# Two half-block products and their sums of the first two up blocks, computed beside the tail's last tiles

## What is computed

```
x = x + rms_norm(mix @ w_out)                       # tail, lane a
u = rms_norm(x)
x = x + rms_norm(cross_attn(u, mem_kv, w_mq, w_mo)) # tail, lanes b, c, d
u = rms_norm(x)                                     # tail, end of lane d: u_T
h = u @ ffn_w_up                                    # ffn: 2 x 2816 columns
c = conv_b + sum(hp[:, k:k + T] * conv_w[k])        # width 3
y = (silu(c[..., :2816]) * c[..., 2816:]) @ ffn_w_down
```

## Time and profile before

| | us |
|---|---|
| median of 3 runs | 3021.24 |
| lowest and highest | 3016.79, 3022.23 |
| the profiled execution, its own time | 3014.63 |
| its span (first to last instruction) | 3012.9 |
| tail stage in the trace | about 1865 to 2147.6 |
| ffn stage in the trace | 2147.6 to about 2717 |

### The profile page before, as it was taken

One profiled execution on the slowest core, in us unless ns is written; L12 is line 12 of the kernel. 1 busy time (PEld: TensorE's weight loads), 2 busy tenths in 40 slices (PEclk: granted clock), 3 DMA queues, 4 the chain that ended last, 5 costly groups with the idle time before them and its releaser, 6 DMA issues. The chain is left out here.

```text
span 3012.9 us, 42602 instructions
## 1 busy us (share of the span) xinstructions
PE 2831.8 (94%) x15048; PEld 1970.8 (65%) x15048; DVE 1307.9 (43%) x2969; ACT 639.2 (21%) x1540; POOL 486.3 (16%) x355
## 2 busy tenths in 40 slices
PE   8999999998989989899999799998699999999998
PEld 5777777765656656566666666555588888874443
DVE  4111123233542597265666344234466666662321
ACT  2111000001322244244444211244111111110010
POOL 1100100003320343100000100011233333320011
PEclk9999999998999999999999899899899999999999
DMA  7644364426983643521111554200234343404020
GB/s 197 138 83 92 90 181 122 133 86 181 261 254 94 176 155 104 183 86 41 46 35 51 179 191 144 83 35 29 80 100 145 109 142 108 146 20 169 2 84 28
DMA packets 343542, 345.04 MB, mean 115 GB/s; under 512 B 61001, under 2 KB 310025, under 8 KB 341982
## 3 DMA queue, kind: packets, MB, share of 16 engines
q1 hardware_dynamic: 298706, 259.32, 29.7%
q10 hardware_dynamic: 44662, 83.46, 8.3%
HBM read 289.37 MB, written 110.01 MB: 133 GB/s over the span
## 5 line engine op out<-in xcount | busy, mean ns | idle before, releaser
L294 PE MATMUL d_ps<-d_w,mixer_u_T 128*128 128x288 f32 (+2 forms) x2048 | 581.4, 431 | 17.7 <-PEq L145 10.3
L294 PEld LDWEIGHTS d_ps<-d_w,mixer_u_T 128*128 128x128 f32 x2048 | 381.6, 193 | 159.0 <-issue 39.2
L298 PE MATMUL d_ps<-mixer_u_T,d_w 128*128 128x352 f32 x1152 | 398.6, 481 | 20.7 <-DVE d_ob L318 11.3
L298 PEld LDWEIGHTS d_ps<-mixer_u_T,d_w 128*128 128x128 f32 x1152 | 208.0, 195 | 127.1 <-issue 39.5
L3376 PE MATMUL ffn_ps<-up_u_T,up_up_w 128*128 128x264 f32 x704 | 163.2, 391 | 2.3 <-DVEq L3509 2.3
L3376 PE MATMUL ffn_ps<-up_u_T,ffn_S 128*128 128x264 f32 x704 | 163.8, 386 | 0.0
L3376 PE MATMUL ffn_ps<-ffn_T,up_up_w 128*128 128x264 f32 x704 | 163.8, 386 | 0.0
L318 DVE COPY d_ob<-d_ps 128x288 f32<-128x288 f32 (+3 forms) x144 | 66.3, 462 | 218.4 <-PE d_ps L294 164.8
L3376 PEld LDWEIGHTS ffn_ps<-up_u_T,up_up_w 128*128 128x128 f32 x704 | 135.7, 193 | 26.4 <-DVEq L3509 2.7
L3070 PE MATMUL down_Y<-down_w,feed_g_T 128*128 128x512 f32 x352 | 151.9, 593 | 0.0
L3376 PEld LDWEIGHTS ffn_ps<-ffn_T,up_up_w 128*128 128x128 f32 x704 | 133.8, 190 | 22.9
(11 more groups left out here) (519 smaller groups left out, 3863.3 us busy)
## 6 DMA issues: line engine op xcount, KB each, us to landing
out_dil_sample<-cache_dil_w ACTq DMA_DIRECT2D x10, 3264.0 KB
up_up_w<-ffn_w_up SPq DMA_DIRECT2D x44, 512.0 KB, 5.2
cmp_rows<-cache_nsa_kv SPq DMA_DIRECT2D x128, 128.0 KB
graw<-d_ob SPq DMA_DIRECT2D x72, 176.0 KB
mix_gate<-graw SPq DMA_DIRECT2D x24, 528.0 KB, 6.0
dils_qb<-proj SPq DMA_DIRECT2D x24, 512.0 KB, 7.4
d_w<-w_in SPq DMA_DIRECT2D x24, 512.0 KB, 6.2
ssd_x<-proj SPq DMA_DIRECT2D x29, 384.0 KB, 4.4
```

The costliest lines, as they stand in the source:

```text
L294: mm = pe.matmul(bank(u)[0:rows, 0:cols], self.u_T[:, k, r0:r0 + rows], self.view(i)[:, k, :], start=(k == 0), stop=(k == DK - 1))
L298: mm = pe.matmul(bank(u)[:, 0:cols], self.view(i)[:, k, x, :], self.u_T[:, k, c * third:(c + 1) * third], start=(k == 0), stop=(k == DK - 1))
```

## The change

In the tail stage, lanes of one step (PE and ACT) are added that make, for blocks 0 and 1 (m = 0, 1), the product P1 (j = 0) of both x into ps_a, copy it to SBUF, then accumulate P2 on top of it (j = 1) and copy the sum P1 + P2. A DVE lane of one step makes two token combinations (T0 and T1 for x = 0), and a POOL lane of four steps makes the four weight combinations of block 0. The results lie in rows of g_T that lane a has finished with. In the ffn stage blocks 0 and 1 skip P1 and P2; block 0 takes its S and the x = 0 input of P6 from the tail's results; the sums C11 become copies; POOL's S of block 0 is gone there, and `clear` stands behind the memsets; the T operations take x = 1 first; the loops of PE, ACT and DVE begin one turn later, with the first turn written out; ACT issues the first turn's two cache transfers ahead of the sigmoid.

```diff
--- before.py
+++ after.py
@@ -3356,11 +3356,13 @@
                                 P5=(lambda slot: A(slot, 1, 0), lambda x: t_of(0, x)), P3=(lambda slot: S[:, 2], lambda x: B(1, 1, x)),
                                 P4=(lambda slot: A(slot, 1, 1), lambda x: t_of(2, x)))
                 weights_made = dict(P6=3, P3=4)
-                inputs_made = dict(P6=(2, 4), P7=(5, 6), P4=(7, 8))
-
-                def block_products(it, slot):
+                inputs_made = dict(P6=(4, 4), P7=(5, 6), P4=(7, 8))
+
+                def block_products(it, slot, begun=False):
                     pe.wait_ge(w_in[slot], it * 32 + 32)
                     for i, (p, x) in enumerate(ORDER):
+                        if begun and p in ("P1", "P2"):
+                            continue
                         q, y = ORDER[(i + RING) % NP]
                         if q == "P1":
                             pe.wait_ge(held, n_of(it, slot, 2, 1 + y))
@@ -3369,16 +3371,26 @@
                             pe.wait_ge(summed, added(it, slot, name) - (NA if i < RING else 0))
                         if p in weights_made:
                             pe.wait_ge(S_made, n_of(it, slot, 4, weights_made[p]))
-                        if p in inputs_made:
+                        lhs, rhs = operands[p]
+                        weights, tokens = lhs(slot), rhs(x)
+                        if begun and slot == 0 and p in ("P6", "P7", "P3"):
+                            weights = begun_weights(g_T)[:, ("P6", "P7", "P3").index(p)]
+                        if begun and slot == 0 and p == "P6":
+                            if x == 0:
+                                tokens = begun_tokens(g_T, 1)
+                            else:
+                                pe.wait_ge(T_made, 2)
+                        elif p in inputs_made:
                             pe.wait_ge(T_made, inputs_made[p][x])
-                        lhs, rhs = operands[p]
                         for k in range(KH):
-                            mm = pe.matmul(bank(p, x)[:, 0:quarter], lhs(slot)[:, k, :], rhs(x)[:, k, :],
+                            mm = pe.matmul(bank(p, x)[:, 0:quarter], weights[:, k, :], tokens[:, k, :],
                                            start=(k == 0), stop=(k == KH - 1))
-                        mm.then_inc(product, 1)
-
-                pe.sem_inc(product, NP)
-                with pe.Fori(0, NB // 2) as it:
+                        mm.then_inc(product, 5 if begun and slot == 0 and (p, x) == ORDER[-1] else 1)
+
+                pe.sem_inc(product, NP + 4)
+                for slot in range(2):
+                    block_products(0, slot, True)
+                with pe.Fori(1, NB // 2) as it:
                     stand(pe, aside)
                     for slot in range(2):
                         block_products(it, slot)
@@ -3405,10 +3417,15 @@
                     for out, cs in parts_of(it * 2 + slot, 0):
                         act.activation(out, cs, ACT.Sigmoid).then_inc(gated, 1)
 
+                act.sem_inc(held, 4)
                 for out, src, n in windows:
                     act.dma_start(out[:, n * TURNS:, :], src[:, n * TURNS:, :]).then_inc(moved, 16)
-                hold(0, 0)
-                with act.Fori(0, TURNS) as it:
+                for out, src, n in windows:
+                    act.dma_start(out[:, 0:n, :], src[:, 0:n, :]).then_inc(moved, 16)
+                gate(0, 0)
+                hold(1, 0)
+                gate(0, 1)
+                with act.Fori(1, TURNS) as it:
                     for out, src, n in windows:
                         act.dma_start(out[:, bass.ds(it * n, n), :], src[:, bass.ds(it * n, n), :]).then_inc(moved, 16)
                     hold(it, 1)
@@ -3435,8 +3452,17 @@
                 def made(it, slot, p, x):
                     dve.wait_ge(product, n_of(it, slot, NP, after(p, x)))
 
-                def first_sums(it, slot):
+                def first_sums(it, slot, begun=False):
                     dve.wait_ge(packed, n_of(it, slot, 2, 2))
+                    if begun:
+                        held_P1, corner = (a.rearrange("p (x c) -> p x c", x=2) for a in begun_sums(g_T, slot))
+                        for x in range(2):
+                            at = pad + quarter * x
+                            dve.tensor_copy(h[:, slot, 0, at:at + quarter], corner[:, x, :]).then_inc(summed, 1)
+                        for x in range(2):
+                            made(it, slot, "P6", x)
+                            add(kept[:, 1, x, :], held_P1[:, x, :], bank("P6", x)[:, 0:quarter])
+                        return
                     for x in range(2):
                         dve.wait_ge(held, n_of(it, slot, 2, 1 + x))
                         made(it, slot, "P2", x)
@@ -3496,9 +3522,9 @@
                         dve.wait_ge(gated, n_of(it, slot, 2, 1 + i))
                         dve.tensor_tensor(out, out, cs, ALU.mult).then_inc(silu, 1)
 
-                def both(now_at, before):
+                def both(now_at, before, begun=False):
                     convolve(*before, 0)
-                    first_sums(*now_at)
+                    first_sums(*now_at, begun)
                     convolve(*before, 1)
                     gate(*before)
                     second_sums(*now_at)
@@ -3507,9 +3533,9 @@
                 dve.sem_inc(st_copied, 1)
                 dve.sem_inc(convolved, 12)
                 dve.sem_inc(summed, NA)
-                for x in range(2):
+                for i, x in enumerate((1, 0)):
                     dve.tensor_tensor(t_of(0, x), B(0, 1, x), B(0, 0, x), ALU.subtract).then_inc(T_made, 1)
-                    dve.wait_ge(T_made, 2 * x + 1)
+                    dve.wait_ge(T_made, 2 * i + 1)
                     dve.tensor_tensor(t_of(1, x), B(1, 1, x), t_of(0, x), ALU.subtract).then_inc(T_made, 1)
                 for x in range(2):
                     dve.tensor_tensor(B(0, 1, x), B(1, 1, x), B(0, 1, x), ALU.subtract).then_inc(T_made, 1)
@@ -3517,10 +3543,12 @@
                 for x in range(2):
                     dve.tensor_tensor(t_of(2, x), B(1, 0, x), t_of(1, x), ALU.subtract).then_inc(T_made, 1)
                 dve.wait_ge(ready, 2)
-                first_sums(0, 0)
+                first_sums(0, 0, True)
                 second_sums(0, 0)
                 states(0, 0)
-                with dve.Fori(0, NB // 2 - 1) as it:
+                both((0, 1), (0, 0), True)
+                both((1, 0), (0, 1))
+                with dve.Fori(1, NB // 2 - 1) as it:
                     both((it, 1), (it, 0))
                     both((it + 1, 0), (it, 1))
                 both((NB // 2 - 1, 1), (NB // 2 - 1, 0))
@@ -3530,7 +3558,6 @@
 
             @block.gpsimd
             def _(pool):
-                clear(nc, pool)
                 def weights(it, slot):
 
                     pool.wait_ge(w_in[slot], it * 32 + 32)
@@ -3559,7 +3586,8 @@
                 pool.sem_inc(multiplied, 2)
                 for slot in range(2):
                     pool.memset(h[:, slot, :, 0:pad], 0.0).then_inc(ready, 1)
-                weights(0, 0)
+                pool.sem_inc(S_made, 4)
+                clear(nc, pool)
                 with pool.Fori(0, NB // 2 - 1) as it:
                     stand(pool, aside)
                     weights(it, 1)
@@ -3578,6 +3606,21 @@
 
     src = ins["cache_mem_kv"][0, b].rearrange("(k j) s h d -> j k s (h d)", j=P)
     eng.dma_start(out, src[:, :, half, :]).then_inc(sem, 16)
+
+
+def begun_sums(g_T, slot):
+
+    return g_T[:, DK + slot, 0:TOK // 2], g_T[:, DK + slot, TOK // 2:TOK]
+
+
+def begun_weights(g_T):
+
+    return g_T[:, DK + 2:DK + 4, :].rearrange("p r t -> p (r t)")[:, 0:3 * DK // 2 * P].rearrange("p (s k n) -> p s k n", s=3, n=P)
+
+
+def begun_tokens(g_T, i):
+
+    return g_T[:, DK + 4 + i, :].rearrange("p (k t) -> p k t", k=DK // 2)
 
 
 def tail(nc, ins, g_T, u_T, up_w, up_in, past, past_in, w_out_in, keys_in, x_first, mem_kv, x_rows, x2, gain_cols, gain_rows, ident):
@@ -4267,8 +4310,70 @@
             sp.wait_ge(stored[RING], 16)
 
         lane_d = Lane(7 * PT, d_pe, d_act, d_dve, d_pool, d_sp)
+
+
+        KH, quarter = DK // 2, TOK // 4
+        begun, begun_copied, begun_steps = st.sem("begun"), st.sem("begun_copied"), st.sem("begun_steps")
+        begun_banks = ps_a[:, :].rearrange("p (x c) -> p x c", x=2)[:, :, 0:quarter]
+
+        def begin_pe(m, j):
+            def program(pe):
+                if m == 0 and j == 0:
+                    pe.wait_ge(made_a, PT)
+                    pe.wait_ge(copied_d, 2 * 5)
+                else:
+                    pe.wait_ge(begun_copied, 2 * m + j)
+                pe.wait_ge(up_in[m], 32)
+                for x in range(2):
+                    for k in range(KH):
+                        mm = pe.matmul(begun_banks[:, x, :], up_w[:, m, KH * j + k, 0, :], u_T[:, KH * j + k, quarter * x:quarter * (x + 1)],
```

(47 more changed lines are left out.)

## The result

| | before, us | after, us |
|---|---|---|
| median of 6 runs each | 3018.26 | 3003.26 |
| lowest and highest | 3011.52, 3022.23 | 2995.14, 3006.97 |
| profiled execution, own time / span | 3014.63 / 3012.9 | 3004.76 / 3003.0 |
| mean granted clock | 0.970 | 0.970 |

The ratio is 0.995, with a 95% interval of 0.9936 to 0.9964: 11 to 19 us faster, 15 in the middle. The range of 2993 to 3009 holds it; the effect is 6 us smaller than the sum of 21.1. The forecast of 3000 us started from a median of 3021.24 over three runs; over six it is 3018.26, and 21.1 less than that is 2997.2. The two spans differ by 9.9 us only, so the first thing to find is how much of that the change made.

What follows compares the result with a forecast made beforehand. PE, 94% busy, was taken to bound the kernel. Terms 18.9 - 0.7 + 1.5 + 1.5 + 0.9 - 1.0 = 21.1 us, against 3021.24, gave a forecast of 3000 us, range 2993 to 3009.

Steps and rivals of the forecast that it cites:

- clock rival: Tail and ffn start: added groups run partly at half clock, clock savings fail; gain 9 to 15 us, chance 0.27.
- the forecast's own case: Whole kernel: the terms hold about as summed, time from 2995 to 3006 us; chance 0.59.
- The ffn stage, 18.9 - 0.7: Ffn start: block 2 starts 18.9 us earlier without 64 records, less 0.7 us for a start not at full clock.
- (c): Tail, gap before 2099.52: filling it keeps the clock, so transposes and queries run faster; +1.5 us, between 0 and 2.
- (d): Tail, behind the second added group: clock held for probability transposes, values and next transposes; 2.3 us whole, +1.5 taken.
- (e): Tail's end: the last eight transposes, right behind the last added group, should take 1.09 us; +0.9 us.
- (f): Tail's end: POOL's residual add waits about 1.0 us for DVE's first added operation at the locked port; -1.0 us.
- the other reading: Tail's end: DVE and POOL share the port equally, so the add lasts as long as both DVE operations; -2.3 us.
- The work came off the path: Answers a rival: DVE's T operations and sums set the ffn start; gain only 6 to 10 us, chance 0.04.
- Block 2's loads: Rival at block 2's start: earlier-requested loads meet ACT's cache copies, PE waits for w_in; kernel slower, chance 0.02.
- its own signs: Forecast wrong if block 2's P1 comes over 41 us after first matmul, clocks near 0.5 remain, or last transposes wait.
- Better than forecast: Tail: both clock savings whole and no port wait; gain of 26 us, about 2995 or less, chance 0.08.

Runs made afterwards that it cites:

- null: The kernel before the change, run again unmodified; 3016.36 us, ratio 0.9991 to 1.0014.
- null2: The kernel before the change, run unmodified once more for its trace; 3020.70 us.
- early_S: Changed kernel, with POOL making block 1's S as soon as T is made instead of behind P3 of block 0; 2999.18 us in a single timed run.
- dve_early: Changed kernel, with DVE's two tail token operations placed before the scaling of y instead of behind it; 3006.33 us in a single timed run.
- fill: Changed kernel plus seven unused matmuls of 248 columns on PE behind the second added group; 2994.85 us in a single timed run.
- one_block: Changed kernel, but only block 0 is begun in the tail and block 1 is made whole in the ffn stage; 3006.22 us, ratio 0.9962.
- tail_only: Kernel before the change plus the four PE groups and their ACT copies in the tail, results unused, ffn stage as before; 3019.72 us, ratio 0.9999.
- again: The changed kernel, run again unmodified; 2999.12 us, ratio 0.9925 to 0.9961.
- padded: Kernel before the change plus 60 semaphore increments each on PE, DVE and SP behind all the work; 3035.7 us.

## Why the prediction was right, and where its sizes were off

**The stretch.** From the w_mo product of 2091.85 on, the sum said 21.1 us, and it is 20.1 against the profile that it was worked out from, 21.4 against the mean of its kernel's three executions. Most of the further 1.3 us come from the last w_mo product, which took 3.67 us in before and 5.6 to 5.8 in null and null2; the sum has no term for it. That the time came within 3 us of the forecast is partly luck, since the median it started from was 3 us too high and the timed gain is 6 us short of the sum. The timed gain of 15 us alone would also fit the upper end of the clock rival (9 to 15); it is the stretch in the traces that speaks for the forecast's own case. By its steps:

- *The ffn stage, 18.9 - 0.7.* The ffn start went from 57.52 to 39.31, 18.21 us where 18.2 was forecast. Two parts of it were off and cancel. Before block 1 PE loses 0.80 us (2177.53, the next start without a break, to 2178.33) and not 0.3 to 0.4. The cause is as forecast, POOL's S behind P3 with only P4 as cover, and the S work takes the 3.85 us of the earlier trace rows (2174.22 to 2178.07). Left out were the two handovers: POOL started 0.25 us behind P3's end at 2173.97, PE 0.26 us behind the third operation's end, so 0.25 + 3.85 + 0.26 - 3.56 = 0.80; early_S takes this wait away. The slow P6 of x = 0 took 3.70 us, half clock, and cost about 0.1 and not the 0.7: the second P6 and P7 have to wait for T anyway, and P7 started 6.3 us behind T's first operation where 6.2 was worked out from the fifth T operation's end. What I took for two terms, the slow P6 and the wait for T, are beside each other and only the later one counts.
- *(c), +1.5.* 1.86 us in after, and the same first half of 19.57 in 6 of the 10 profiled kernels with the change or part of it; in the other four it is 0.2 to 0.5 against before and nothing against null and null2, with queries of 4.88 to 5.46 us. The gap is filled in all ten, and the row of dve_early shows the queries slow behind the same 2.05 us as in after:

```profile
2113.43 0.66 PE L4159 MATMUL tail_T_c<-const_ident,tail_probs 128*128 128x128 f32 x4 [2.05 <-DVE tail_probs L4187]
2114.03 5.46 PE L4126 MATMUL tail_T_b<-tail_u,tail_w_mq 128*128 128x128 f32 x32
```

  Right in mechanism, but an execution may not get it: over the ten, the first half is 1.0 us shorter than over the three profiles of the kernel before (20.15 against 21.14), less than the 1.5 of the sum.
- *(d), +1.5.* **This is the step that failed.** Second half 19.15 to 19.03: 0.1 us where 1.5 were booked, or 0.4 against null and null2. The first transposes gave back 0.45 us, the last ones lost 0.32, and second transposes and values gained nothing. The 3.15 us of gap left behind (0,1) were named as the risk and then priced too low. What fill shows goes further than that: filled to 0.22 us, the clock still fell. Its windows:

```profile
2124.00:2126.00 2.00, 0.99 (x8) 0.70 (x8) 0.98 (x4) 1.80 (x5) 0.00 (x0) 1.00 0.59 246
2126.00:2128.00 2.00, 1.32 (x15) 1.09 (x15) 0.91 (x2) 1.00 (x2) 0.00 (x0) 0.82 0.00 0
2128.00:2130.00 2.00, 2.00 (x14) 1.67 (x12) 0.00 (x0) 0.37 (x1) 0.00 (x0) 0.50 0.00 0
```

  Between 2124 and 2128 PE did eight transposes and the first value matmuls, 2.3 us of work with gaps of 0.79 and 0.68 us, and then ran at half clock without a gap. This is the rule weighed in the prediction as a rival's ground (the Trainium skill, TensorE: Matmul & The Clock Gate, "Part 4: PE-mode transpose": transposes do not hold the full clock as matmuls do); the windows agree with it, but don't part the transposes from the short gaps among them.
- *(e), +0.9.* The last transposes take 1.09 instead of 1.97 us: 0.88, and one_block, without the last pair, has the 1.97 back. They waited for x_n and not for (1,1).
- *(f), -1.0.* 0.95 us, and dve_early gives just that back. It was rows 7 that had the answer: an operation waits out the whole of the other's. By the other reading, an equal share, it would have been 2.3. The Trainium skill's lock (SBUF — State Buffer, "SBUF: two separate sides") agrees with 3.29 against 2.34 us.
- (e) and (f) cancel: the tail's end is 15.72 before and 15.80 after.
- *The rivals.* The work came off the path: tail_only and one_block both show it (nothing for the records in the gaps, 6.34 us for 32 of them in the stage). Block 2's loads are not late; PE runs from 2178.33 to the end of the products without a gap. The clock rival holds for (d), for the stage's first P6 (3.70 us, at a cost of about 0.1) and in some executions for (c). By its own signs the forecast was wrong on this point: clocks of 0.63 and 0.52 stand in the windows behind the second group, and the values took 2.03 us and not 1.1. Its other two signs stayed away: P1 of block 2 came 39.3 us after the stage's first matmul (the limit was 41), and the last transposes didn't wait for (1,1).
- *A sum of the prediction.* "Better than forecast" was put at a gain of 26 us. Its own terms, (c) and (d) whole and no wait for the port, give 21.1 + 0.45 + 0.8 + 1.0 = 23.4, and 24.1 with the start of the ffn stage at full clock. It did not come about either way.

**What is open.** The stretch gained 21.4 us and the timed runs 15.1 and 17.2 (0.5% and 0.57% of 3017). again's interval reaches from 11.8 to 22.6 us and holds 21.4, after's ends at 19.3 and doesn't. Behind block 2 nothing was lost (805.6 to 807.2 us in every kernel but padded), so in the traces what is missing lies ahead of the last tiles. There the kernels with the change arrived at 2092.9 to 2106.5 (mean 2099.5 of ten), those of the kernel before at 2089.6 to 2097.6 (mean 2093.0 of three), in code that is the same. That is 6.5 us, and 21.4 - 6.5 = 14.9 would be about the timed gain; but single executions of one kernel differ by more, as the 309.1 and 299.9 us of after and again above show. Whether this is a shift or only scatter was not settled; padded, at 2105.99, leans to a shift that has to do with the program and not with this change's work, and one execution can't carry that.

## What to carry to other kernels

Read the gain of a local change between two products that both traces have; the spans alone said 9.9 us here where this stretch gained 20 to 21 and the timed runs 15 to 17, and one execution of before differed from the next by 8 us where nothing had been touched. Report the timed gain beside it, since the two need not agree. Work put into an engine's gap is free if it ends before the old releaser does (64 records, 14.2 us, cost nothing), but don't book the clock that it keeps while gaps remain on the way to the next long product; here even a fill that left no more than 0.8 us at once gave back only 0.7 of the 1.9 us hoped for. When work moves out of a stage, look at once for what it had covered there: here POOL's S lost its cover, and a start that needn't have waited for P3 gave 0.87 us back.

## What the runs showed of the hardware

**The clock can fall with PE busy.** The timeline of PE in null has 63 records of 16 columns in 8.94 us, again has the same in 11.28:

```profile
1893.80 8.94 PE L3829 MATMUL tail_T_c<-tail_x_n,up_up_w 128*128 128x16 f32 x63
```

```profile
1902.60 11.28 PE L3872 MATMUL tail_T_c<-tail_x_n,up_up_w 128*128 128x16 f32 x63
```

and the windows of again show the engine busy for 2.00 of 2 us and 4.00 of 4 us while the granted clock falls to half:

```profile
1902.00:1904.00 2.00, 2.00 (x16) 1.61 (x14) 0.00 (x0) 0.00 (x0) 0.00 (x0) 1.00 0.00 0
1904.00:1906.00 2.00, 2.00 (x16) 2.00 (x16) 0.00 (x0) 0.00 (x0) 0.00 (x0) 0.79 0.00 0
1906.00:1910.00 4.00, 4.00 (x20) 4.00 (x20) 0.00 (x0) 0.00 (x0) 0.00 (x0) 0.50 0.00 0
```

In null it fell later in the same sequence (0.73 between 1898 and 1900). That is 2.3 us of difference for the same instructions, and so one part of the scatter.

**The same code doesn't always get the same clock.** With the same group ahead and the same 2.05 us gap, the queries took 3.84 us in six kernels' traces and 4.88 to 5.46 in four; the w_mo product behind a gap of 1.47 us took 3.67 us in ten traces and 5.58 to 5.77 in the other four (null, null2, padded and tail_only).
